# Attention of a hybrid decoder step: value products four units behind the scores, turns of `o` one round later, a negated maximum, q scaled in its copy

## The chip, the cores and the metric

The kernel runs on one core of a Trainium2 chip, as one program. The metric is the device time of one execution in microseconds. Three executions are given as their median. The chip has a matmul engine (TensorE, PE in the profile), a vector engine (VectorE, DVE), a scalar engine (ScalarE, ACT), a general one (GpSimd, POOL) and a queue engine (SyncE, SP) that issues most transfers. Each engine runs its own list of instructions in order; they wait for each other on semaphores.

## The reference

One inference step of a decoder with two layers, for a prompt of 1,024 tokens and 8 sample tokens. Layer A is an RWKV-7 mixing and an MLP; behind it shared keys and values are projected; layer B is a differential attention over them and an MLP. The part that matters here is the attention:

```python
def diff_combine(s, lam):
    p = jax.nn.softmax(s, axis=-1)
    return p[..., 0, :, :] - lam * p[..., 1, :, :]
# prompt: for each block i of 128 queries, 8 heads, two key maps of 64 each
s = jnp.einsum('bqhmd,bkhmd->bhmqk', qi, k).astype(jnp.float32) * ATTN_SCALE
s = jnp.where(k_pos[None, :] <= q_pos[:, None], s, NEG)
attn = diff_combine(s, lam).astype(v.dtype)
o = jnp.einsum('bhqk,bkhe->bqhe', attn, v)
# samples: one query each over 1,024 keys gathered by a page table, and the new key
on = of * lax.rsqrt(jnp.mean(jnp.square(of), -1, keepdims=True) + SUBLN_EPS) * g * (1.0 - lam_init)
```

`ATTN_SCALE` is 64 ** -0.5, that is 1/8, an exact power of two. All is float32.

## The kernel before, in words

The program is a row of phases with a barrier of all engines between them: start, projections, scan, sample scan, dense phase of layer 0 (which also projects k, v and q for the attention and writes them to a scratch in memory), attention, dense phase of layer 1. The change touches the dense phase in one place and `attention_phase`.

In the dense phase each projected tile of k, v or q (128 x 344) is copied out of PSUM by ACT at L1807 and sent to the scratch. There are 72 such copies, 24 of them of q.

In `attention_phase` the work of the prompt is cut into 64 units: unit u is head u // 8 and the query block `ORDER[u % 8]`, with `ORDER = (7, 0, 6, 1, 5, 2, 4, 3)`. A unit of block i has i + 1 key blocks of 128. So even units are long (8, 7, 6, 5 key blocks) and odd units short (1, 2, 3, 4), and each pair has nine. u % 8 is called r, the round within a head. Long and short units have PSUM and SBUF buffers of their own. All engines run the same loop over u, from 0 to `END` (74), and each does in round u what belongs to it:

- PE, round u: turn (transpose) the first four blocks of the combined attention of unit w = u - `LAG` (`turn4`, L2233), with `LAG = 3`; the scores of unit u (L2251) with the causal mask added by a matmul (L2255); the turn of the other blocks of w; the value products of w (`values`, L2265); and the extras of u.
- DVE, round u: the maximum of the scores of u (`maxima`, L2405) and, from it, the negated and scaled maximum `nb` (L2407); a page sum (L2424); `combine` of unit u - 1 (L2413, L2415, and the scalar_tensor_tensor L2419, which gives map 0 plus a ratio times map 1); in odd rounds a second page sum. At r = 5 the finished `o` of the head before is scaled (L2443).
- ACT, round u: copies of the turned blocks of w out of PSUM (`turned`, L2529), mixed with the two exponentials of unit u - 1 (`exps`, L2521, bias `nb`, scale 1/8, and the sum of the row); the copies of the extras; the copy of the value products of w into `o` (`take`, L2536) and its sum of squares (L2539). At r = 4 the square root for the head before (L2594), which needs a table load each way.
- POOL, round u: products of a page of sample keys with a query row (L2223), 64 pages in rounds 0 to 42, three in two rounds (one in an even round, two in an odd one). The first of a round waits until DVE has combined unit u - 2.
- SP: loads of key pages, of value pages, and of query rows (`q_row`, L2172), in order of rounds.

The extras (`extras`) are the remaining turns that go through the one turning bank of PSUM (`tb`): the rows of the next head's k and v at r = 2 to 5 ("rows"); the turns of the scaled `o` of the head before ("fin", two halves, L2233 on PE, L2550 on ACT), at r = 6 and 7 of the next head; the page scores (L2283) and what follows for the two halves of the samples, at u = 22 and 43 and some rounds behind; and the products with value pages (L2308, L2315) at eight values of u from 28 to 58. Each user of the bank waits until ACT has copied what the one before it put there; `nth` numbers them in the order of the loop.

```python
for u in range(END):
    w = u - LAG
    for i in range(2):
        for name in attn_rounds(w)[i:i + 1]:
            turned(name)
        if 1 <= u <= NU:
            exps(u - 1, (i,))
    for name in extras(u):
        extra(name)
    if 0 <= w < NU:
        take(w)
```

This is ACT's loop (L2579 to L2589).

## Time and profile before

| | |
|---|---|
| median of three runs | 3,694.8 us (3,684.2 to 3,699.2) |
| profiled execution | 3,698.0 us |
| its span | 3,696.2 us |
| PE busy | 3,319.3 us (90%) |
| DVE busy | 1,960.4 us (53%) |
| ACT busy | 1,443.6 us (39%) |
| POOL busy | 1,756.3 us (48%) |
| attention phase | from about 2,370 to 2,815 us of the span |

The profile is of one execution, taken by the hardware. Times in it count from the start of the span. "L2407" is line 2407 of the kernel. A busy share is a mean over phases with different limits, so each stage has to be read by itself. A row of waits says which engine and line stood idle and which instruction ended that, as far as semaphores tell it.

### The profile page before, as it was taken

How to read it: one execution, taken by the hardware profiler on the slowest of the kernel's cores; microseconds unless marked ns; L12 is line 12 of the kernel's file. 1: busy time of each engine (PE TensorE's matmuls, PEld its weight loads, DVE VectorE, ACT ScalarE, POOL GpSimd, SP SyncE). 2: the span in 40 equal slices, each digit the busy share in tenths (PEclk: the TensorE clock that was granted, in tenths of full speed). 3: DMA queues.
4: the chain of work that ended last, by engine and by line, in shares of the span. 5: the costliest groups of instructions: out<-in, count | busy, mean ns of one | idle time of the engine just before them, and what ended most of it. 6: DMA issues, size and time to landing. Idle time of an engine off the chain costs nothing. (4 is left out here: it accounts for less than half of the span.)

```text
span 3696.2 us, 78976 instructions
## 1 busy us (share of the span) xinstructions
PE 3319.3 (90%) x34073; PEld 3076.8 (83%) x34073; DVE 1960.4 (53%) x2233; ACT 1443.6 (39%) x2357; POOL 1756.3 (48%) x716
## 2 busy tenths in 40 slices
PE   7999879999985499999999999777886999999997
PEld 6889668888884499999999999654555999999997
DVE  6985264555532675673344342298744746742432
ACT  3433324433331234343333343355654443433332
POOL 3676410001000266666667666464402667666663
PEclk8999979999996699999999999888888999999998
DMA  8556533433432544545445566568755444444442
GB/s 289 173 168 181 171 109 114 133 129 112 133 96 61 183 136 132 143 139 153 140 140 155 156 199 188 179 225 272 276 180 161 132 137 143 137 144 140 138 146 84
DMA packets 784518, 575.27 MB, mean 156 GB/s; under 512 B 45306, under 2 KB 747666, under 8 KB 783916
## 3 DMA queue, kind: packets, MB, share of 16 engines
q1 hardware_dynamic: 728356, 506.07, 44.6%
q10 hardware_dynamic: 55816, 64.16, 5.3%
q8 instruction: 270, 4.42, 0.5%
q14 instruction: 76, 0.62, 0.1%
HBM read 499.86 MB, written 70.29 MB: 154 GB/s over the span
## 5 line engine op out<-in xcount | busy, mean ns | idle before, releaser
L1702 POOL TENSOR_TENSOR dense_w_lo<-w_raw,dense_w_hi 128x1024 fp32r<-128x1024 f32 x504 | 1290.8, 2566 | 985.4 <-ACT dense_w_hi L1785 985.2
L1754 PE MATMUL acc<-dense_x_hi,dense_w_hi 128*128 128x344 f32 x2496 | 792.7, 322 | 27.2 <-DVE dense_x_lo L1891 21.0
L1755 PE MATMUL acc<-dense_x_lo,dense_w_hi 128*128 128x344 f32 x2496 | 788.3, 320 | 0.0
L1785 ACT ACTIVATE dense_w_hi<-w_raw 128x1024 fp32r<-128x1024 f32 x504 | 530.6, 1056 | 510.6 <-PE acc L1759 443.8
L1754 PEld LDWEIGHTS acc<-dense_x_hi,dense_w_hi 128*128 128x128 f32 x2496 | 470.5, 188 | 33.5 <-DVE dense_x_lo L1891 16.6
L1754 PE MATMUL acc<-dense_hid_hi,dense_w_hi 128*128 128x344 f32 x1536 | 487.2, 322 | 0.0
L1755 PE MATMUL acc<-dense_hid_lo,dense_w_hi 128*128 128x344 f32 x1536 | 483.4, 319 | 0.0
L1755 PEld LDWEIGHTS acc<-dense_x_lo,dense_w_hi 128*128 128x128 f32 x2496 | 470.8, 189 | 0.6
L1759 PE MATMUL acc<-dense_x_hi,dense_w_lo 128*128 128x344 f32 x2496 | 447.2, 321 | 2.2 <-POOL dense_w_lo L1702 2.2
L1759 PEld LDWEIGHTS acc<-dense_x_hi,dense_w_lo 128*128 128x128 f32 x2496 | 407.2, 189 | 2.7 <-POOL dense_w_lo L1702 2.7
L797 POOL TENSOR_TENSOR x0T<-nT,levels 128x512 f32<-128x512 f32 x16 | 29.7, 1856 | 592.6 <-DVE bR L1296 592.6
L1907 DVE TENSOR_TENSOR dense_relu<-dense_relu 128x344 f32<-128x344 f32 x192 | 124.0, 646 | 338.7 <-ACT dense_relu L1801 338.7
L478 POOL TENSOR_TENSOR proj_w_lo<-proj_w_raw,proj_w_hi 128x1024 fp32r<-128x1024 f32 (+1 forms) x84 | 229.6, 2744 | 135.1 <-ACT proj_w_hi L598 82.2
L1754 PEld LDWEIGHTS acc<-dense_hid_hi,dense_w_hi 128*128 128x128 f32 x1536 | 288.5, 188 | 1.6
L1755 PEld LDWEIGHTS acc<-dense_hid_lo,dense_w_hi 128*128 128x128 f32 x1536 | 288.3, 188 | 1.6
L1759 PE MATMUL acc<-dense_hid_hi,dense_w_lo 128*128 128x344 f32 x1536 | 274.2, 321 | 0.0
L1801 ACT ACTIVATE dense_relu<-acc 128x344 f32<-128x344 f32 x192 | 88.0, 458 | 455.9 <-PE acc L1759 428.6
L1759 PEld LDWEIGHTS acc<-dense_hid_hi,dense_w_lo 128*128 128x128 f32 x1536 | 249.6, 188 | 0.0
L1926 DVE SCALAR_TENSOR_TENSOR z<-acc,mods,z 128x344 f32<-128x344 f32 (+1 forms) x144 | 81.0, 567 | 300.3 <-PE acc L1759 300.3
L506 PE MATMUL acc<-proj_x_hi,proj_w_hi 128*128 128x344 f32 (+2 forms) x672 | 214.3, 323 | 13.2 <-ACT proj_w_hi L598 8.8
L2223 POOL TENSOR_TENSOR att_k_prod<-att_k_page,att_q_row_all 128x1024 f32<-128x1024 f32 x64 | 150.1, 2359 | 154.8 <-DVE att_attn_short L2419 66.7
L507 PE MATMUL acc<-proj_x_lo,proj_w_hi 128*128 128x344 f32 (+2 forms) x672 | 213.6, 322 | 0.0
(406 smaller groups left out, 6097.1 us busy)
## 6 DMA issues: line engine op xcount, KB each, us to landing
w_raw<-in_ffn_w SPq DMA_DIRECT2D x384, 512.0 KB, 4.2
ada_quarter<-in_ada_w SPq DMA_DIRECT2D x40, 1024.0 KB, 10.9
proj_w_raw<-in_a_w_rkv SPq DMA_DIRECT2D x72, 512.0 KB, 4.1
att_k_page<-in_cache_k SPq DMA_DIRECT2D x64, 512.0 KB, 4.2
att_v_page<-in_cache_v SPq DMA_DIRECT2D x64, 512.0 KB, 6.0
scratch_mix<-proj_stage ACTq DMA_DIRECT2D x72, 344.0 KB, 3.1
scratch_mix<-dense_stage ACTq DMA_DIRECT2D x72, 172.0 KB, 2.1
w_raw<-in_a_w_o SPq DMA_DIRECT2D x24, 512.0 KB, 4.4
```

The costliest lines, as they stand in the source:

```text
L478: nc.gpsimd.tensor_tensor(wlo[:, s % NW, :, 0:w], raw[:, s % NRAW, :, 0:w], whi[:, s % NW, :, 0:w].bitcast(F32), ALU.subtract).then_inc(S( ...
L506: T_.matmul(out, whi[:, s % NW, k, 0:w], xh[x][:, k, :], start=k == 0, stop=False)
L507: T_.matmul(out, whi[:, s % NW, k, 0:w], xl[x][:, k, :], start=False, stop=False)
L1702: nc.gpsimd.tensor_tensor(wlo[:, i % NW], raw[:, i % NRAW], whi[:, i % NW].bitcast(F32), ALU.subtract).then_inc(S("lo"), 1)
L1754: T_.matmul(out, whi[:, s % NW, k, :], a, start=j.first and k == 0, stop=False)
L1755: T_.matmul(out, whi[:, s % NW, k, :], b, start=False, stop=False)
L1759: last = T_.matmul(out, wlo[:, s % NW, k, :], a, start=False, stop=j.last and k == KC - 1)
L1785: A(whi[:, i % NW], raw[:, i % NRAW], ACT.Copy).then_inc(S("hi"), 1)
L1801: A(t[:, n % 2, :], bank(jobs[s].acc), ACT.Relu).then_inc(S("taken"), 1)
L1907: V.tensor_tensor(tt, tt, tt, ALU.mult).then_inc(S("hid_sq"), 1)
L1926: V.scalar_tensor_tensor(zk, ps[:, 0:w], m.mod(gt, j.mo), zk, ALU.mult, ALU.add).then_inc(S("added"), 1)
L2223: nc.gpsimd.tensor_tensor(prod[:, j % NR, :], kp[:, j % NK, :], qb[:, b % 2, :], ALU.mult).then_inc(S("prod"), 1)
```

## The change

Four edits:

1. `LAG` goes from 3 to 4: turns and value products of a unit stand four rounds behind its scores.
2. The turns of the scaled `o` move from rounds 6 and 7 to round 7 and round 0 of the head after.
3. The maximum is written negated by the reduce itself, so the tensor_scalar that scaled and negated it, the buffer between them and its two factors go; the same for the samples' page scores.
4. q is multiplied by 1/8 when ACT copies it out of PSUM in the dense phase; the exponentials lose their scale.

```diff
--- before.py
+++ after.py
@@ -1804,7 +1804,7 @@
                     n = sum(1 for i in jobs[0:s] if i.kind in "kvq")
                     need(act, "mm", s + 1)
                     need(act, f"out{n % NOUT}", 16 * (n // NOUT))
-                    A(stage[:, n % NOUT, :], bank(j.acc), ACT.Copy).then_inc(S("taken"), 1)
+                    A(stage[:, n % NOUT, :], bank(j.acc), ACT.Copy, scale=ATTN_SCALE if j.kind == "q" else 1.0).then_inc(S("taken"), 1)
                     act.wait_ge(S("taken"), count[s])
                     nc.scalar.dma_start(m.scr[row[j.kind], j.mo, :, j.g * G:(j.g + 1) * G], stage[:, n % NOUT, :]
                                         ).then_inc(S(f"out{n % NOUT}"), 16)
@@ -2030,7 +2030,7 @@
         NK, NV, NR = 4, 12, 3
         GS, GR = NS // 2, NS // 2 * 16
         SM, VU = (22, 43), (28, 32, 36, 40, 49, 52, 55, 58)
-        END, LAG = NU + 10, 3
+        END, LAG = NU + 10, 4
         q, k, v = sb("q", [P, 2, SEQ]), sb("k", [P, 2, SEQ]), sb("v", [P, SEQ])
         krow, vrow = sb("k_rows", [P, KC, P]), sb("v_rows", [P, 2, KC, P])
         causal, mask, eyer = sb("causal", [P, P]), sb("causal_r", [P, P], F32R), sb("eye_r", [P, P], F32R)
@@ -2038,9 +2038,8 @@
         at = (sb("attn_long", [P, 2, SEQ]), sb("attn_short", [P, 2, SEQ // 2]))
         aT = (sb("attn_cols_long", [P, SEQ]), sb("attn_cols_short", [P, SEQ // 2]))
         o, osq, outT = sb("o", [P, 2, KC, P]), sb("o_sq", [P, P]), sb("out_cols", [P, SEQ])
-        mx, nb, l, rl, w1 = (sb(x, [P, 4, 2]) for x in ("max", "neg_max", "sums", "weights", "ratio"))
+        nb, l, rl, w1 = (sb(x, [P, 4, 2]) for x in ("neg_max", "sums", "weights", "ratio"))
         ss, rs, sums2 = sb("ss", [P, KC]), sb("rms", [P, KC]), sb("square_sums", [P, 2, KC])
-        factor = sb("score_factor", [P, 2])
         lq, eps, gcol = sb("lam_rows", [P, 2, P]), sb("eps", [P, 2]), sb("subln_g", [P, 2])
         ls, lam = sb("lam_sums", [P, 2]), sb("neg_lambda", [P, 1])
 
@@ -2108,8 +2107,10 @@
             out = []
             if 2 <= r <= 5 and h + 1 < NH:
                 out.append(("rows", h + 1, r - 2))
-            if r >= 6 and 1 <= h <= NH:
-                out.append(("fin", h - 1, r - 6))
+            if r == 7 and 1 <= h <= NH:
+                out.append(("fin", h - 1, 0))
+            if r == 0 and 2 <= h <= NH + 1:
+                out.append(("fin", h - 2, 1))
             g = group(u, 0)
             if g is not None:
                 out += [("page_sc", g, 0), ("page_sc", g, 1), ("page_new", g, 0)]
@@ -2367,9 +2368,6 @@
             V.tensor_copy(mask[:], causal[:]).then_inc(S("consts"), 1)
             V.tensor_copy(eyer[:], m.ident[:]).then_inc(S("consts"), 1)
             V.memset(eps[:, 0:1], SUBLN_EPS)
-            V.memset(factor[:, 0:1], -ATTN_SCALE).then_inc(S("factor"), 1)
-            V.memset(factor[:, 1:2], 1.0).then_inc(S("factor"), 1)
-            need(dve, "factor", 2)
             V.memset(eps[:, 1:2], P * SUBLN_EPS).then_inc(S("consts"), 1)
             V.memset(ones[:], 1.0)
             for i in range(4):
@@ -2402,9 +2400,7 @@
             def maxima(u):
                 c = u % 4
                 need(dve, "s_mm", u + 1)
-                V.tensor_reduce(mx[:, c, :], both_scores(u), AX.X, ALU.max).then_inc(S("max"), 1)
-                need(dve, "max", u + 1)
-                V.tensor_scalar(nb[:, c, :], mx[:, c, :], factor[:, 0:1], factor[:, 1:2], ALU.mult, ALU.mult).then_inc(S("nb"), 1)
+                V.tensor_reduce(nb[:, c, :], both_scores(u), AX.X, ALU.max, negate=True).then_inc(S("nb"), 1)
 
             def combine(u):
                 kd, c, n = kind(u), u % 4, blocks(u) * P
@@ -2445,9 +2441,7 @@
                 g = group(u, 1)
                 if g is not None:
                     need(dve, "t_in", nth["page_new", g, 0] + 1)
-                    V.tensor_reduce(pmx[0:GR, :], pr[0:GR, :], AX.X, ALU.max).then_inc(S("page_nb"), 1)
-                    need(dve, "page_nb", 2 * g + 1)
-                    V.tensor_scalar(pmx[0:GR, :], pmx[0:GR, :], -ATTN_SCALE, None, ALU.mult).then_inc(S("page_nb"), 1)
+                    V.tensor_reduce(pmx[0:GR, :], pr[0:GR, :], AX.X, ALU.max, negate=True).then_inc(S("page_nb"), 1)
                 g = group(u, 2)
                 if g is not None:
                     need(dve, "page_exp", g + 1)
@@ -2518,7 +2512,7 @@
                 need(act, "nb", u + 1)
                 need(act, "attn", u - 1)
                 for mp in maps:
-                    A(pm[kd][:, mp, 0:n], scores_of(u, mp), ACT.Exp, bias=nb[:, c, mp:mp + 1], scale=ATTN_SCALE,
+                    A(pm[kd][:, mp, 0:n], scores_of(u, mp), ACT.Exp, bias=nb[:, c, mp:mp + 1],
                       accum_out=l[:, c, mp:mp + 1]).then_inc(S("exp"), 1)
 
             def turned(name):
@@ -2594,8 +2588,8 @@
                     A(ss[:], sums2[:, (h - 1) % 2, :], ACT.Sqrt, bias=eps[:, 0:1], scale=1.0 / P).then_inc(S("rms"), 1)
                 g = group(u, 1)
                 if g is not None:
-                    need(act, "page_nb", 2 * g + 2)
-                    A(pr[0:GR, :], pr[0:GR, :], ACT.Exp, bias=pmx[0:GR, 0:1], scale=ATTN_SCALE, accum_out=pl[0:GR, 0:1]).then_inc(S("page_exp"), 1)
+                    need(act, "page_nb", g + 1)
+                    A(pr[0:GR, :], pr[0:GR, :], ACT.Exp, bias=pmx[0:GR, 0:1], accum_out=pl[0:GR, 0:1]).then_inc(S("page_exp"), 1)
             for name in ("k_out", "v_out", "mix_out"):
                 act.wait_ge(S(name), 16 * NH)
```

PE at the turn of `o` of head 1, rounds 22 and 23 (`att_attn_long` and `_short` are the combined attention of long and short units, `att_scores` the page scores, `att_o` the scaled `o`). Before:

```order
L2251 MATMUL acc<-att_k,att_q 128x512 x2
L2251 MATMUL acc<-att_k,att_q 128x128 x2
L2255 MATMUL acc<-att_causal_r,att_eye_r 128x128 x2
L2233 MATMUL aux<-ident,att_o 128x128 x4
L2265 MATMUL aux<-att_v_rows,att_attn_cols_short 128x128 x2
L2283 MATMUL aux<-ident,att_scores 64x128 x8
L2297 MATMUL aux<-att_ones,att_new_prod 64x1
L2233 MATMUL aux<-ident,att_attn_long 128x128 x4
L2251 MATMUL acc<-att_k,att_q 128x512 x2
L2255 MATMUL acc<-att_causal_r,att_eye_r 128x128 x2
```

After the change:

```order
L2252 MATMUL acc<-att_k,att_q 128x512 x2
L2252 MATMUL acc<-att_k,att_q 128x128 x2
L2256 MATMUL acc<-att_causal_r,att_eye_r 128x128 x2
L2234 MATMUL aux<-ident,att_attn_long 128x128 x3
L2266 MATMUL aux<-att_v_rows,att_attn_cols_long 128x128 x4
L2284 MATMUL aux<-ident,att_scores 64x128 x4
L2266 MATMUL aux<-att_v_rows,att_attn_cols_long 128x128 x3
L2284 MATMUL aux<-ident,att_scores 64x128 x4
L2298 MATMUL aux<-att_ones,att_new_prod 64x1
L2234 MATMUL aux<-ident,att_attn_short 128x128 x2
L2252 MATMUL acc<-att_k,att_q 128x512 x2
L2256 MATMUL acc<-att_causal_r,att_eye_r 128x128 x2
L2234 MATMUL aux<-ident,att_o 128x128 x4
```

The turn of `att_o` went from behind the scores of round 22 (512 and 128 columns) to behind those of round 23 (512 columns); the page scores now stand between the value products of a long unit, and the long scores of round 22 stand with long turns where they stood with short ones.

DVE in round 2 and the start of round 3. Before:

```order
L2405 TENSOR_REDUCE att_max<-acc 128x2
L2407 TENSOR_SCALAR att_neg_max<-att_max,att_score_factor 128x2
L2424 TENSOR_REDUCE att_scores<-att_k_prod 128x16
L2413 RECIPROCAL att_weights<-att_sums 128x2
L2415 TENSOR_SCALAR att_ratio<-att_weights,att_sums,att_neg_lambda 128x1
L2419 SCALAR_TENSOR_TENSOR att_attn_short<-att_probs_short,att_ratio 128x128
L2405 TENSOR_REDUCE att_max<-acc 128x2
L2407 TENSOR_SCALAR att_neg_max<-att_max,att_score_factor 128x2
```

After the change:

```order
L2403 TENSOR_REDUCE att_neg_max<-acc 128x2
L2420 TENSOR_REDUCE att_scores<-att_k_prod 128x16
L2409 RECIPROCAL att_weights<-att_sums 128x2
L2411 TENSOR_SCALAR att_ratio<-att_weights,att_sums,att_neg_lambda 128x1
L2415 SCALAR_TENSOR_TENSOR att_attn_short<-att_probs_short,att_ratio 128x128
L2403 TENSOR_REDUCE att_neg_max<-acc 128x2
L2420 TENSOR_REDUCE att_scores<-att_k_prod 128x16
```

The reduce writes `att_neg_max` itself, and one instruction of a unit is gone; the order of the others is the same.

ACT in rounds 11 and 12 (`att_k_rows` is the copy of an extra). Before:

```order
L2529 ACTIVATE att_attn_cols_long<-aux 128x512
L2521 ACTIVATE att_probs_long,att_sums<-acc,att_neg_max 128x896
L2529 ACTIVATE att_attn_cols_long<-aux 128x512
L2521 ACTIVATE att_probs_long,att_sums<-acc,att_neg_max 128x896
L2503 ACTIVATE att_k_rows<-aux 128x512
L2512 DMA out_k_prompt<-att_k_rows 128x8x128
L2536 ACTIVATE att_o<-aux,att_weights 128x128
L2539 ACTIVATE att_o_sq,att_square_sums<-att_o 128x128
L2529 ACTIVATE att_attn_cols_short<-aux 128x128
L2521 ACTIVATE att_probs_short,att_sums<-acc,att_neg_max 128x256 x2
```

After the change:

```order
L2523 ACTIVATE att_attn_cols_short<-aux 128x512
L2515 ACTIVATE att_probs_long,att_sums<-acc,att_neg_max 128x896 x2
L2497 ACTIVATE att_k_rows<-aux 128x512
L2506 DMA out_k_prompt<-att_k_rows 128x8x128
L2530 ACTIVATE att_o<-aux,att_weights 128x128
L2533 ACTIVATE att_o_sq,att_square_sums<-att_o 128x128
L2523 ACTIVATE att_attn_cols_long<-aux 128x512
L2515 ACTIVATE att_probs_short,att_sums<-acc,att_neg_max 128x256
L2523 ACTIVATE att_attn_cols_long<-aux 128x512
L2515 ACTIVATE att_probs_short,att_sums<-acc,att_neg_max 128x256
```

Before, the copies of long turned blocks stood between long exponentials and the short copy before short ones; now the short copy stands before the long exponentials, and the long copies between short ones.

## Rows read from the trace of the kernel before

**Rows 1.** Busy time by stretch: busy us and instructions of each engine, PE clock, DMA.

```profile
2390.00:2430.00 40.00, 30.94 (x164) 21.80 (x164) 39.20 (x48) 21.22 (x61) 25.96 (x12) 0.79 0.65 220
2430.00:2480.00 50.00, 36.88 (x197) 25.79 (x197) 47.09 (x58) 30.91 (x81) 28.04 (x12) 0.83 0.65 219
2730.00:2780.00 50.00, 44.45 (x295) 30.00 (x296) 23.97 (x42) 29.20 (x81) 0.00 (x0) 0.90 0.51 161
```

**Rows 2.** Groups and waits of the attention phase: busy, mean ns; waited us, times, longest us.

```profile
L2407 DVE TENSOR_SCALAR att_neg_max<-att_max,att_score_factor 128x2 f32<-128x2 f32 x64 | 43.2, 674 | 2.3
...
DVE att_max L2405 <- PE acc L2255: 18.8, 9, 6.1
...
PE aux L2233 <- DVE att_o L2443: 14.1, 3, 7.9
...
DVE att_max L2405 <- PE acc L2255: 54.0, 15, 7.7
...
PE aux L2233 <- ACT att_attn_cols_long L2529: 8.0, 5, 3.4
...
PE aux L2233 <- DVE att_o L2443: 1.0, 1, 1.0
```

**Rows 3.** Timeline, units 11 to 13: start, us, engine, line, out<-in [idle before <-releaser].

```profile
2449.19 1.21 DVE L2424 TENSOR_REDUCE att_scores<-att_k_prod 128x16 f32<-128x1024 f32 x1
...
2450.32 1.74 DVE L2405 TENSOR_REDUCE att_max<-acc 128x2 f32<-128x1536 f32 x1
...
2452.10 0.29 DVE L2407 TENSOR_SCALAR att_neg_max<-att_max,att_score_factor 128x2 f32<-128x2 f32 x1
2452.30 1.21 DVE L2424 TENSOR_REDUCE att_scores<-att_k_prod 128x16 f32<-128x1024 f32 x1
...
2454.58 4.66 POOL L2223 TENSOR_TENSOR att_k_prod<-att_k_page,att_q_row_all 128x1024 f32<-128x1024 f32 x2 [2.79 <-DVE att_attn_short L2419]
...
2455.31 1.64 DVE L2407 TENSOR_SCALAR att_neg_max<-att_max,att_score_factor 128x2 f32<-128x2 f32 x1
...
2456.96 1.22 DVE L2424 TENSOR_REDUCE att_scores<-att_k_prod 128x16 f32<-128x1024 f32 x1
...
2458.60 1.46 DVE L2419 SCALAR_TENSOR_TENSOR att_attn_long<-att_probs_long,att_ratio 128x768 f32<-128x768 f32 x1
```

**Rows 4.** Timeline, units 22 and 23.

```profile
2513.70 1.12 PE L2233 MATMUL aux<-ident,att_o 128*128 128x128 f32 x4 [7.85 <-DVE att_o L2443]
...
2517.70 4.64 POOL L2223 TENSOR_TENSOR att_k_prod<-att_k_page,att_q_row_all 128x1024 f32<-128x1024 f32 x2 [5.13 <-DVE att_attn_short L2419]
...
2523.67 1.23 DVE L2405 TENSOR_REDUCE att_max<-acc 128x2 f32<-128x1024 f32 x1 [6.14 <-PE acc L2255]
...
2526.76 0.88 DVE L2419 SCALAR_TENSOR_TENSOR att_attn_long<-att_probs_long,att_ratio 128x640 f32<-128x640 f32 x1
```

**Rows 5.** Timeline, units 27, 28 and 30.

```profile
2552.39 1.65 DVE L2407 TENSOR_SCALAR att_neg_max<-att_max,att_score_factor 128x2 f32<-128x2 f32 x1
...
2554.08 0.47 ACT L2521 ACTIVATE att_probs_short<-acc,att_neg_max 128x256 f32<-128x256 f32 x1 [2.10 <-DVE att_neg_max L2407]
...
2555.64 1.92 PE L2308 MATMUL aux<-att_v_page,att_page_attn 128*32 128x512 f32 x16 [2.14 <-ACT att_v_rows L2508]
...
2574.72 1.49 DVE L2405 TENSOR_REDUCE att_max<-acc 128x2 f32<-128x1280 f32 x1 [2.33 <-PE acc L2255]
```

**Rows 6.** Query rows: issue on SP's queue, and POOL's products behind them.

```profile
2500.81 0.43 SPq L2172 DMA_DIRECT2D att_q_row_all<-scratch_sample_y  x1
...
2507.89 4.67 POOL L2223 TENSOR_TENSOR att_k_prod<-att_k_page,att_q_row_all 128x1024 f32<-128x1024 f32 x2 [2.52 <-issue]
...
2589.43 2.36 POOL L2223 TENSOR_TENSOR att_k_prod<-att_k_page,att_q_row_all 128x1024 f32<-128x1024 f32 x1 [5.90 <-DMA att_q_row_all<-scratch_sample_y]
```

**Rows 7.** Timeline, unit 42.

```profile
2654.84 2.02 DVE L2405 TENSOR_REDUCE att_max<-acc 128x2 f32<-128x1792 f32 x1 [2.08 <-PE acc L2255]
```

**Rows 8.** The copies of k, v and q out of PSUM, by tile.

```profile
L1807 ACT ACTIVATE dense_stage<-acc x72: 435/457/459, 2086.6 to 2356.1; 128x344 f32<-128x344 f32 x72
```

## The prediction

> **What bounds the kernel now.** I read the instruction times around the changed lines first. All of the change but one scale factor lies in the attention phase, from about 2,370 to 2,815 us of the span. Then the busy time by stretch [rows 1]: from 2,390 to 2,480 us DVE is busy 86.3 of 90 us, while PE has 67.8. From 2,730 to 2,780 us it is the other way round: PE 44.5 of 50, DVE 24.0. So there are two regimes. Units 1 to 42, while the sample group's pages are multiplied on POOL and summed on DVE, are limited by DVE; units 43 to 63 by PE together with ACT, which empties PE's one turning bank.
>
> The waits [rows 2] say where each regime leaks. With pages, DVE waits 18.8 us for scores, and PE waits 14.1 us for the scaled `o` (three times, 7.9 us at the longest). Without pages DVE waits 54.0 us for scores, but PE waits only 8.0 us for the turned long columns on ACT and 1.0 us for `o`: DVE's wait there is spare time.
>
> The timeline of units 11 to 13 [rows 3] shows what ends DVE's idle time inside its own instructions. The tensor_scalar on L2407 has 2 elements a partition. In unit 12 it takes 0.29 us. In unit 13 it takes 1.64 us, from 2,455.31 to 2,456.95, and POOL's product, begun at 2,454.58, lasts half of 4.66 us, to 2,456.91. The combine of unit 12 (L2419, 768 elements) starts at 2,458.60 and ends at 2,460.06, after POOL's second product (2,459.24). So a DVE operation of this kind does not run beside a product; it ends after it. And the page sum (L2424) at 2,456.96 reads that very product.
>
> **The change, part by part.** The profiled execution took 3,698.0 us, its span 3,696.2; the sum is made against 3,698.0, 3.2 above the median of 3,694.8.
>
> *The negated maximum* removes 64 instructions of L2407, 43.2 us of busy time, 674 ns each [rows 2]. The upper bound is all of that, if DVE were the limit everywhere and nothing took its place. The lower is zero. What stays depends on the unit. In an even unit (long scores) the product was finished before, so the page sum moves up. It starts 1.98 us after a 1.74 us reduce at 2,450.32 [rows 3]; after an instruction that it need not wait for, a reduce starts 0.08 us before the other's end (1.13 us behind one of 1.21, at 2,449.19). Without L2407 that is 1.66, a gain of 0.3 us. In an odd unit DVE waits for the same product with or without the tensor_scalar, and its next combine waits for POOL's second one: no gain on DVE. There `nb` comes 1.4 to 2 us earlier, which only ACT sees. There are 21 even units with pages. In five of them (10, 16, 20, 32, 36) the gain is taken back by the query row that POOL needs for the next sample: it is issued only after the last product but one. Issued at 2,500.81 it is followed by POOL's product at 2,507.89, 7.1 us later, and at 2,589.43 POOL had waited 5.9 us on it [rows 6]. That leaves 16 x 0.3 = **4.8 us**. In the last 21 units DVE has 54 us spare [rows 2]: 0.
>
> The Trainium skill (SBUF — State Buffer, two separate sides) says that DVE and GpSimd hold their common pair of ports under a lock for a whole instruction and the loser "fully blocks". By that rule the trace agrees (1.64 us instead of 0.29). Its plain reading would let the blocking vanish with the blocked instruction; that is rival E.
>
> *The later turns of `o`*. In unit 22 PE waits until 2,513.70 with the first half, then still has values, page scores and a turn to do, and the scores of unit 23 reach DVE at 2,523.67, after 6.14 us of idle time [rows 4]. After the change the first turn stands behind the scores of unit 23, and those can be done before 2,517.5. POOL's two products (from 2,517.70, 4.64 us) still end at 2,522.34, and the combine, which took until 2,527.64, then ends 0.9 us behind them, at 2,523.3: **4.3 us**. Unit 15 had the same wait with 1.9 us, but there POOL's products and the next query row end at the same time as before: 0.2. In the last 21 units the wait was 1.0 us [rows 2]: **1.0**.
>
> *One more unit between scores and values*. (a) The turn no longer waits for the combine; in the DVE regime that only moves PE's idle time. (b) Pairing: before, ACT had long turns and long exponentials in the same round, now long turns meet short exponentials, and PE gets long scores with long turns. Work is the same, so I take a third of the 8.0 us that PE waited for the long columns in the last 21 units [rows 2]: **2.7 us**. Ends: -3 (if PE's light rounds now wait for ACT instead) and 8. (c) The end of the phase has one unit more to drain, about 2 us of PE work, and the scores of unit 63 stand as much earlier: 0.
>
> *Both together, at page products of PE*. In unit 27 `nb` ends at 2,554.04 behind POOL; ACT waits 2.10 us for it, PE 2.14 us for ACT, and the chain of page values behind it runs into DVE at unit 30, which waits 2.33 us [rows 5]. With `nb` 1.6 us earlier that is **1.6 us**. Units 39, 41 and 42 wait 0.7, 1.3 and 2.1 us for scores (the last in [rows 7]); half of that, **2.1**. Unit 37 gains 0.7, as POOL's query row is late there.
>
> *q scaled in ACT's copy* (24 of the 72 of L1807, 457 ns each [rows 8]): the same instruction with another constant, so 0; each waits for PE anyway. Two memsets and a wait at the start go: POOL's first row is what is waited for: 0.
>
> Sum: 4.8 + 4.3 + 0.2 + 1.0 + 2.7 + 1.6 + 2.1 + 0.7 = 17.4 us, 3,698.0 to 3,680.6; against the median, **3,677.4 us**, 0.5% faster.
>
> **The rivals.**
> *A, handed back.* The gains before unit 32 end in waits for query rows and pages, and PE's light rounds wait for ACT as long as before. For it: the 5.9 us on a query row [rows 6], which no part of the change issues earlier. Against it: unit 23 has no such wait behind it. It leaves unit 23 and part of the even units, 4.3 + 2.7 = 7 us: 3,688.
> *B, PE gets faster too.* The granted clock was 0.79 to 0.83 with pages and 0.90 without [rows 1], of levels at 1.2 and 2.4 GHz, and PE had stood idle for up to 7.9 us before the slow pieces. If PE idles less and 0.90 becomes 0.97 in the 135 us after unit 43, of which PE is busy nine tenths, that is 0.07 x 120 = 8 us; with all 8.0 instead of 2.7 us of waits, 5 more: 31 us in all, 3,664. The Trainium skill (TensorE: Matmul & The Clock Gate, Part 1) ties the half clock to an idle PE; the low figure beside the 7.9 us wait fits that. Against it: the page values make PE wait for ACT in any order.
> *C, slower.* PE has its long scores, turns and values now in the same round. In units 43 to 63 the odd unit's scores come some 1.5 us later (four turns, up to eight value matmuls), while ACT's long exponentials, which follow them, hold the turning bank's next copy. If neither is made up in the even round, 10 pairs x 1.5 = 15 us are lost; where pages meet them too, only the 4.8 us of the even units stay: 10 us slower, 3,705. It decides once DVE, with 54 us spare in 135, uses that up; that speaks against it.
> *E, the blocking goes.* The 43.2 us hold 64 x 0.29 = 18.6 us of work and 24.7 us of waiting for POOL. If DVE could use the odd units' share, the time would be 3,677 - 25 = 3,653. Against it: the page sum of 2,456.96 needs the product that ended at 2,456.91 [rows 3].
> *D, it does nothing*, because every removed wait had another behind it: 3,695.
>
> **How the numbers follow.** Forecast 0.47, A 0.22, B 0.15, C 0.07, D 0.06, E 0.03. A measurement of this kernel tells about 0.5%, 18.5 us, from no change. The forecast lies just inside it: with its bounds (12 to 24 us) it is over in 0.20 of its 0.47, and B and E are over, so faster 0.38. C gives slower 0.05, the rest is 0.57. The range goes from B to between D and A: **3,663 to 3,692**.
>
> **What would show it.** Right: L2407's group gone and DVE busy some 40 us less; in units 22 and 23 no wait of PE for `o` over 1 us and unit 23's reduce within 5 us of unit 22's combine; in odd units with pages the page sum still begins as POOL's product ends, in even ones 0.3 us sooner after the reduce; query rows still waited for. Wrong: a time under 3,664 with the page units shorter by far more than 13 us, which means the blocking did go; or new waits of DVE for odd scores after unit 43.

## The result, and the profile after

The changed kernel took **3,705.5 us** (median of 15 runs, 3,690.7 to 3,711.7), the kernel before, measured beside it, 3,690.8 (15 runs, 3,680.5 to 3,699.2): ratio 1.0027, 95% interval 1.0014 to 1.0039, so 5 to 14 us slower, a small difference but clear of the interval. The forecast was 3,677.4, and the time lies outside its range. The profiled execution took 3,707.4 us with a span of 3,705.6.

The length of the attention phase says more than the whole time. I count it from unit 0's maximum to the next phase's first operation on POOL, and cut it at the maxima of units 22, 43 and 63. First the kernel before, in this cut (columns: stretch, its length, busy us and instructions of PE, PE's weight load, DVE, ACT, POOL, then PE's granted clock as a share of 2.4 GHz (0.50 is the half clock), DMA share, GB/s):

```profile
2374.60:2513.60 139.00, 98.26 (x521) 67.40 (x518) 121.62 (x146) 77.51 (x201) 79.46 (x34) 0.81 0.73 243
2513.60:2659.00 145.40, 119.82 (x727) 78.01 (x727) 118.84 (x149) 83.22 (x219) 70.69 (x30) 0.86 0.84 305
2659.00:2792.30 133.30, 109.72 (x683) 72.58 (x683) 63.23 (x117) 83.29 (x213) 0.00 (x0) 0.88 0.41 133
2792.30:2816.60 24.30, 9.94 (x63) 8.16 (x61) 6.42 (x13) 11.99 (x31) 0.00 (x0) 0.78 0.14 45
```

The changed kernel, same view and cut:

```profile
2382.60:2517.50 134.90, 92.59 (x518) 64.39 (x516) 100.13 (x124) 76.20 (x198) 80.11 (x34) 0.81 0.77 251
2517.50:2660.90 143.40, 117.17 (x709) 78.92 (x708) 102.12 (x126) 81.39 (x216) 71.42 (x30) 0.83 0.86 311
2660.90:2798.20 137.30, 112.10 (x695) 74.90 (x694) 57.89 (x96) 82.64 (x214) 0.00 (x0) 0.86 0.38 127
2798.20:2827.40 29.20, 12.45 (x74) 10.16 (x72) 6.12 (x12) 15.25 (x37) 0.00 (x0) 0.76 0.12 38
```

442.0 us became 444.8. The first two stretches won 4.1 and 2.0 us, the third lost 4.0, the drain (what is left to do behind unit 63's maximum) lost 4.9. L2407 is gone, as forecast (page: DVE 1,960.4 us busy before, 1,905.2 after, 55 less where some 40 were expected). Behind unit 22 this helped little or not at all, and PE's clock fell there: 0.86 and 0.88 became 0.83 and 0.86.

Attention began 8.0 us later, at 2,382.6, though nothing ahead of it is changed but a factor in the copies of q. From 1,320 us of the first trace to the last of these copies the distance of the two traces stays 8.3 us, so the copies themselves are no slower with the factor.

The local steps of the forecast are there. DVE's waits for scores in the stretch with pages (up to unit 43's maximum) and in the one without, against [rows 2]:

```profile
DVE att_neg_max L2403 <- PE acc L2256: 27.0, 11, 4.6
...
DVE att_neg_max L2403 <- PE acc L2256: 60.6, 19, 7.4
```

No wait of PE for `o` is left in either stretch (14.1 us in three [rows 2]), but DVE waits for scores 27.0 us instead of 18.8 with pages, and 60.6 us in 19 waits instead of 54.0 in 15 without: the new waits after unit 43 that the prediction named as a sign of being wrong. Units 22 and 23, against [rows 4]:

```profile
2517.49 1.48 DVE L2403 TENSOR_REDUCE att_neg_max<-acc 128x2 f32<-128x1280 f32 x1
...
2521.30 4.67 POOL L2224 TENSOR_TENSOR att_k_prod<-att_k_page,att_q_row_all 128x1024 f32<-128x1024 f32 x2 [4.81 <-DVE att_attn_short L2415]
...
2521.78 0.62 PE L2234 MATMUL aux<-ident,att_o 128*128 128x128 f32 x4
...
2521.98 1.23 DVE L2403 TENSOR_REDUCE att_neg_max<-acc 128x2 f32<-128x1024 f32 x1 [0.85 <-PE acc L2256]
...
2525.32 1.33 DVE L2415 SCALAR_TENSOR_TENSOR att_attn_long<-att_probs_long,att_ratio 128x640 f32<-128x640 f32 x1
```

The 6.14 us wait is 0.85 us, and the turn of `o` comes at the full clock (0.62 us, before 1.12). In unit 12 the page sum starts 1.66 us after the reduce (1.98 before), just as forecast. In odd units POOL's product ends the page sum's wait, where L2407 used to sit, as forecast from [rows 3] (unit 13):

```profile
2459.79 4.66 POOL L2224 TENSOR_TENSOR att_k_prod<-att_k_page,att_q_row_all 128x1024 f32<-128x1024 f32 x2 [2.47 <-DVE att_attn_short L2415]
2462.17 1.22 DVE L2420 TENSOR_REDUCE att_scores<-att_k_prod 128x16 f32<-128x1024 f32 x1 [1.68 <-POOL att_k_prod L2224]
```

### The profile page after: what moved, and what is told of

Same layout as the page of the kernel before. It is cut to its first block and busy times, and to the rows that moved or that the text cites. A ratio compares the mean times of both kernels' runs of the same rounds, so it can differ in the third digit from the quotient of the medians.

```text
span 3705.6 us, 78908 instructions
## 1 busy us (share of the span) xinstructions
PE 3323.2 (90%) x34073; PEld 3083.7 (83%) x34073; DVE 1905.2 (51%) x2165; ACT 1443.0 (39%) x2357; POOL 1758.4 (47%) x716
## 5 line engine op out<-in xcount | busy, mean ns | idle before, releaser
L478 POOL TENSOR_TENSOR proj_w_lo<-proj_w_raw,proj_w_hi 128x1024 fp32r<-128x1024 f32 (+1 forms) x84 | 228.8, 2735 | 139.8 <-ACT proj_w_hi L598 85.4
```

What stands on the lines that cost most here:

```text
L478: nc.gpsimd.tensor_tensor(wlo[:, s % NW, :, 0:w], raw[:, s % NRAW, :, 0:w], whi[:, s % NW, :, 0:w].bitcast(F32), ALU.subtract).then_inc(S( ...
```

## The experiments

Twelve edited kernels, and a second profile of the kernel before, of the changed one and of the changed one with three units. "Before" in the ratios was run beside each. "Half clock", in us, is worked out from the granted clock in stretches of 2 us: two times (1 - clock) times the length, summed; where the stretches begin shifts it by up to 2 us. "PE busy" and "half clock" are those of units 22 to 63.

| kernel | ratio to before (95%) | attention | units 0-22 | 22-43 | 43-63 | drain | PE busy 22-63 | half clock 22-63 |
|---|---|---|---|---|---|---|---|---|
| before | 1 | 442.0 | 139.0 | 145.4 | 133.3 | 24.3 | 229.5 | 72.5 |
| before, again | | 442.6 | 139.8 | 146.2 | 131.1 | 25.5 | 228.8 | 69.9 |
| changed | 1.0027 (1.0014-1.0039) | 444.8 | 134.9 | 143.4 | 137.3 | 29.2 | 229.3 | 85.4 |
| changed, again | | 445.4 | 135.5 | 143.4 | 137.3 | 29.2 | 229.2 | 85.4 |
| negated maximum alone | 0.998 (0.997-0.9991) | 428.2 | 136.0 | 139.5 | 127.2 | 25.5 | 223.4 | 55.8 |
| turns of o alone | 0.9967 (0.9949-0.9984) | 427.3 | 137.9 | 138.0 | 126.0 | 25.4 | 218.3 | 58.1 |
| four units alone | 1.002 (1.0011-1.003) | 451.1 | 138.3 | 145.0 | 137.3 | 30.5 | 231.0 | 87.2 |
| changed, three units | 0.9961 (0.9947-0.9974) | 422.7 | 137.3 | 133.6 | 127.3 | 24.5 | 216.7 | 52.7 |
| changed, three units, again | | 419.5 | 135.5 | 132.7 | 126.1 | 25.2 | 214.5 | 51.3 |
| changed, five units | 0.9985 (0.997-0.9999) | 433.6 | 134.4 | 133.0 | 132.0 | 34.2 | 218.7 | 54.6 |

Two theories to begin with: 1, the fourth unit costs; 2, the phases ahead of attention were made longer.

**The parts apart.** `lag3_in_after`:

```diff
-        END, LAG = NU + 10, 4
+        END, LAG = NU + 10, 3
```

> The changed kernel with three units between scores and values again; the negated maximum, the scaled q and the later turns of o stay. Theory 1 (the fourth unit costs: units 37 to 63 lost 7 us against before, and the drain behind the last combine lasts 12.2 instead of 7.2 us): the attention phase becomes 10 to 14 us shorter than in the changed kernel, the drain is 7.2 us again, and the time is 5 to 12 us below the kernel before, ratio 0.997 to 0.999. Theory 2 (the loss lies in the 8 us by which the phases ahead of attention were longer, through the scaled copy of q or through where the instructions lie): these stay, and the time is that of the changed kernel less the 5 us of the drain, ratio 1.001 to 1.002.

Measured: 14 us faster than before, more than theory 1 wanted; attention 22 us shorter than changed (expected 10 to 14). Only the drain missed theory 1: by its count, from the last combine to the reciprocal, 8.4 us instead of 7.2. `lag4_alone` is the opposite edit (3 to 4) in the kernel before:

> The kernel before with four units between scores and values, nothing else. Theory 1: 8 to 14 us slower than before (drain 5, the last 27 units 7, nothing won with pages), ratio 1.002 to 1.004; unit 63's scores and all of units 43 to 63 come late by some 0.3 us a unit. Theory 2: only the drain's 5 us, and the phases ahead of attention as in the kernel before: ratio 1.0013.

7.4 us slower, and 8.8 us more attention (451.1 against 442.3, the mean of the two profiles before), 5.6 of them in the drain: about what theory 1 expected. `fin_alone` takes only the hunk of `extras` into the kernel before:

> The kernel before with only the two turns of o one round later. Both theories: unit 23's scores are no longer waited for 6 us, which was worth 5.6 us in the changed kernel; 3 to 6 us faster than before, ratio 0.9985 to 0.999. If the query rows hand it back, 0 to 2 us.

It won 12 us by the ratio and 15 in attention: twice the upper end of what was expected, and more than twice the forecast's 5.5 us. `max_alone` is the changed kernel with LAG 3 and the old hunk of `extras`:

> The kernel before with only the maximum written negated and q scaled in its copy. Theory 1: 3 to 6 us faster than before, all of it by unit 42, nothing after; phases ahead of attention unchanged within a few us of scatter. Theory 2: if the scaled copy of q (or the code's place) makes the phases ahead of attention longer, they are 5 to 8 us longer than in the kernel before, and the time is 2 to 4 us slower.

7 us faster, attention 14 us shorter. So two of the three parts are good. The third loses more than both win, but only beside them: changed with three units against changed is 22 to 26 us of attention, where the same edit in the kernel before cost 8.8. What the fourth unit mostly does is to take back what the other two won. About half of their excess over the forecast stands in units 43 to 63, for which the forecast had 0 and 1.0 us: 127 and 126 us instead of 131 and 133.

**Scatter.** Both kernels, unedited, once more:

> The kernel before, profiled once more, to see how far two executions of one program lie apart stage by stage. If the phases ahead of attention scatter by themselves, they differ by up to 10 us from the first profile (2,376.9 us), and the 8 us by which the changed kernel came to attention later are scatter. In the attention phase (439.7 us in the first) theory 1 wants 430 to 442 us.

> The changed kernel, profiled once more. Theory 1: the attention phase (443.3 us in the first profile) is again over 440 us, and TensorE's time at half clock in units 43 to 63 again near 38 us (it was 17 to 24 us in the three kernels that keep three units and carry one or both of the other parts).

Attention repeats to 0.7 us in both, that of the kernel with three units to 3.2 (its second profile, below). The phases ahead of it do not: attention began at 2,374.6 and 2,384.7 us in one kernel, 2,382.6 and 2,377.1 in the other. The 8 us are no more than this scatter. Over all profiles attention begins at 2,378.3 us in the mean of the four without the scaled q and at 2,377.7 in that of the thirteen with it; theory 2 falls. (The two expectations count attention from later operations, 2.3 and 1.5 us behind unit 0's maximum; by this count it took about 440 and 444 us, inside theory 1's bands.) In the changed kernel units 43 to 63 have 37.6 us at half clock both times, as expected.

**Parity or distance.** The busy time of PE differs by 13 us between three and four units, for the same instructions. With three units, long turns meet short scores; with four, long scores; with five, short ones again. `lag5`, with row buffers of the sums and weights for eight units:

```diff
-        END, LAG = NU + 10, 4
+        END, LAG = NU + 10, 5
-        nb, l, rl, w1 = (sb(x, [P, 4, 2]) for x in ("neg_max", "sums", "weights", "ratio"))
+        nb, l, rl, w1 = (sb(x, [P, 8, 2]) for x in ("neg_max", "sums", "weights", "ratio"))
...
-                need(dve, "take", u - 3)
+                need(dve, "take", u - 7)
```

> The changed kernel with five units between scores and values (row buffers of the sums for eight units). Turned values of a long unit then stand beside the scores of a short one again, as with three. Theory P (what costs is that long turns, long scores and long values share a round, parity): units 43 to 63 take 126 to 130 us as with three units, TensorE is at half clock 17 to 26 us of it, the drain becomes 17 us; time 5 to 12 us below the changed kernel. Theory Q (more distance itself costs, whatever the parity): 137 us or more, drain 17 us, time 5 to 15 us above the changed kernel.

Units 22 to 43 took 133.0 us as with three, so distance itself costs nothing there. Units 43 to 63 took 132.0, between the theories, with 31 us at half clock instead of 17 to 26. The drain grew by five more: 24.9, 29.2, 34.2 us with three, four, five units. In all, five units won back 11.5 us of the 24 of attention. `lag5` also has deeper row buffers, but these were not what cost: in the changed kernel DVE's waits in units 22 to 63 end with scores, exponentials, products of POOL and once, after 0.2 us, its own ratio, never with a value product, its copy or a turn.

**Page steps.** Where the page steps stand, four units put the extra steps of the page group beside a short unit. One round later they meet a long one again:

```diff
-        SM, VU = (22, 43), (28, 32, 36, 40, 49, 52, 55, 58)
+        SM, VU = (23, 44), (29, 33, 37, 41, 50, 53, 56, 59)
```

> The changed kernel (four units) with the steps of the sample group's page values and of its page scores one round later each (table of rounds 23, 44 and 29, 33, 37, 41, 50, 53, 56, 59), so that they meet a unit of the same kind between turns as they did with three. Length of attention is counted here from unit 0's maximum to the next phase's first operation on POOL: 442.0 and 442.6 us before, 444.8 and 445.5 changed, 422.7 with three units. Theory P (with four, page steps meet the light round of a short unit; PE waits 2 to 4.5 us there and its clock stays at half through the long round that follows): units 22 to 63 take 262 to 270 us instead of 280.7, half clock 55 to 65 instead of 85 us, the drain stays at 29; attention 427 to 434 us. Theory Q (four units cost by the long turns and long scores in one round, wherever the page steps stand): 278 us or more, attention 442 to 448.

> As above, but only the page values' rounds are later by one. Theory P: units 28 to 42 and 49 to 60 gain (together 5 to 12 us against the changed kernel), the loss at units 45 to 47 behind the page scores' exponential (8 us against three units) stays. Theory Q: nothing over 3 us.

> The reverse: three units, and the page steps one round later. Theory P: the page steps now meet short units there, and attention is 6 to 15 us longer than 422.7 us (with three units and the old rounds), with more than 65 us of half clock in units 22 to 63. Theory Q: within 4 us of 422.7.

| kernel | ratio (95%) | attention | 0-22 | 22-43 | 43-63 | drain | PE busy 22-63 | half clock |
|---|---|---|---|---|---|---|---|---|
| pages later | 0.9996 (0.9982-1.0011) | 438.6 | 135.5 | 142.3 | 133.3 | 27.5 | 217.7 | 57.8 |
| values later (one run) | | 438.8 | 136.1 | 139.6 | 134.0 | 29.2 | 220.4 | 66.6 |
| three units, pages later (one run) | | 431.1 | 135.5 | 142.3 | 128.3 | 25.0 | 222.8 | 71.4 |
| four, then three units | 0.9998 (0.9981-1.0015) | 437.4 | 135.3 | 142.7 | 135.1 | 24.3 | 227.5 | 77.3 |

The direction is theory P's both times: 6 us better with four units, 8 to 12 worse with three. The size is theory P's with three units only; with four, attention stays above its 427 to 434 us. In pages_later PE's half clock came down as expected and its busy time with it, but its idle time rose from 51.4 to 57.9 us. Moving the page values alone won as much (438.8 us; 5.3 us in units 28 to 42, 0.5 in 49 to 60). So where the steps stand is a quarter to a half of the loss, not the whole. `lag4_then_3` returns to three units once the pages are done (of its diff only the table of units is shown):

```diff
+        def units_of(u):
+            return [u - 4] if u < 43 else [39, 40] if u == 43 else [u - 3]
```

> The changed kernel with four units up to round 42, two units' values in round 43, and three from there. Theory P: units 22 to 43 stay at 143 us, units 43 to 63 fall from 137 to 127 to 131 us, the drain from 29.2 to 24.5; attention 430 to 434 us, 12 to 15 us below the changed kernel. If the loss after unit 43 came from what the page part left behind, units 43 to 63 stay at 135 us or more and only the drain's 5 us come back.

The drain's 5 us came back, but units 43 to 63 took 135.1 us: as it was put, theory P missed, and the other reading, something left behind by the page part, is not refuted. A reading made afterwards speaks against it. Round 43 does two units, and unit 44 is 4.1 us later than in the changed kernel; from there to unit 63 this kernel lost 2.4 us against the first profile with three units, the changed kernel 8.9. No run separates the two.

**Waits or clock.** Where does PE's busy time go? This is PE in the changed kernel, units 29 and 30:

```profile
2569.24 3.57 PE L2316 MATMUL aux<-att_fold,att_page_o 128*128 128x1 f32 x16 [2.73 <-ACT att_v_rows L2502]
...
2573.17 1.09 PE L2234 MATMUL aux<-ident,att_attn_long 128*128 128x128 f32 x4 [0.36 <-ACT att_res L2565]
...
2574.19 2.51 PE L2252 MATMUL acc<-att_k,att_q 64*128 64x512 f32 x8
```

PE waits 2.73 us behind a short unit's two value matmuls, and then everything up to the long scores runs at 1.2 GHz: 16 one-column matmuls 3.57 us, four turns 1.09, the long scores 2.51. The single wait does not decide it. With three units the waits just ahead of the same column matmuls are 0.86 and 1.34 us in both profiles, and the matmuls took 3.41 us in one and 2.17 in the other; the two units took 16.7 and 14.8 us, a large part of what these two profiles differ by. In the changed kernel PE waits like this ahead of the columns in units 29 and 37 (2.73 and 2.07 us) and once later, in unit 53; in units 24 and 45 it waits 4.5 and 3.9 us. `filled` puts matmuls whose result nobody reads into units 24 and 45, in a free part of the value bank:

```diff
+                if group(u, 2) is not None:
+                    need(pe, "take", w)
+                    for i in range(5):
+                        T_.matmul(ob[:, P:4 * P], m.ident[:], k[:, (u // KC) % 2, 0:3 * P], start=True, stop=True)
```

> The changed kernel with five matmuls of 384 columns (about 3.2 us at the full clock, results unused) on TensorE in units 24 and 45, where it waits 3.9 us for ACT's exponential of the page scores. Theory C (the fall of the clock behind the wait costs): in unit 45 to 47, which were at 0.60 and 0.71, the clock stays above 0.9, and units 45 to 48 become 3 to 5 us shorter; time 3 to 8 us below the changed kernel. Theory W (the wait costs and the clock does not matter): those units are as long or 0 to 3 us longer, the time not shorter.

`filled_more` adds four of them before the page columns where r = 5:

```diff
+                    if name[0] == "page_cols" and u % KC == 5:
+                        for i in range(4):
+                            T_.matmul(ob[:, P:4 * P], m.ident[:], k[:, (u // KC) % 2, 0:3 * P], start=True, stop=True)
```

> As the kernel filled, and four more unused matmuls of 384 columns ahead of the page columns in units 29, 37 and 53, where TensorE with four units waits 2.7, 2.1 and 2.7 us for ACT's copy of v's rows. Theory C (waits cost through the clock behind them): the two stretches at half clock behind units 29 and 37, 10 and 13 us long, shrink by more than half, units 29 to 45 become 3 to 6 us shorter than in filled, TensorE's busy time for the program's own work falls with them; attention 435 to 439 us. Theory W (only the waits count): units 29 to 45 as in filled (142.8 us for units 22 to 43) or longer by up to 1.5 us.

> The changed kernel with three units and with the five unused matmuls in units 24 and 45, where TensorE still waits 3.7 and 3.4 us. Theory C: half clock in units 22 to 63 falls from 52.7 to 35 to 45 us and attention from 422.7 to 417 to 421 us, ratio to before 0.994 to 0.996. Theory W: 422 to 425 us.

> The changed kernel with three units, profiled once more: attention within 1 us of 422.7 us if the phase repeats as the other two kernels' did (442.0 and 442.6; 444.8 and 445.5), and units 22 to 63 with 50 to 56 us of half clock.

| kernel | ratio (95%) | attention | 0-22 | 22-43 | 43-63 | drain | PE busy 22-63 | half clock |
|---|---|---|---|---|---|---|---|---|
| filled | 0.9989 (0.9972-1.0006) | 441.8 | 134.9 | 142.9 | 136.5 | 27.5 | 230.7 | 71.6 |
| filled more | 0.9978 (0.996-0.9997) | 432.5 | 135.7 | 136.0 | 133.3 | 27.5 | 226.7 | 40.9 |
| three units, filled | 0.9959 (0.9943-0.9975) | 421.0 | 135.6 | 133.2 | 127.8 | 24.4 | 219.9 | 42.3 |

The same three steps in filled_more:

```profile
2554.12 2.75 PE L2368 MATMUL aux<-att_k,ident 128*128 128x384 f32 x8
...
2557.02 1.95 PE L2316 MATMUL aux<-att_fold,att_page_o 128*128 128x1 f32 x16
...
2559.32 0.63 PE L2234 MATMUL aux<-ident,att_attn_long 128*128 128x128 f32 x4 [0.36 <-ACT att_res L2572]
2559.88 1.35 PE L2252 MATMUL acc<-att_k,att_q 64*128 64x512 f32 x8
```

Units 29 and 30 as a whole, in filled and in filled_more (one row each):

```profile
2561.90:2578.20 16.30, 12.34 (x64) 9.62 (x65) 10.70 (x14) 9.08 (x25) 3.28 (x2) 0.69 0.95 334
```

```profile
2552.50:2565.20 12.70, 11.26 (x71) 8.14 (x72) 10.60 (x13) 9.09 (x25) 3.30 (x2) 1.00 0.91 314
```

More work, and 3.6 us sooner. Units 45 and 46, in the changed kernel and in filled:

```profile
2674.70:2693.00 18.30, 12.83 (x56) 8.79 (x57) 7.30 (x14) 12.34 (x31) 0.00 (x0) 0.65 0.11 30
```

```profile
2671.60:2685.90 14.30, 11.42 (x67) 7.38 (x66) 7.09 (x14) 11.82 (x30) 0.00 (x0) 1.00 0.14 38
```

4.0 us shorter, at the full clock (units 45 to 47 together 18.5 us instead of 22.9, as theory C expected). In unit 24 the filling brought next to nothing. The clock rose from 0.57 to 0.96 there, but what PE won ended in a wait of 2.13 us for DVE's weighted page scores, and in unit 25 the clock was 0.50 both times. Units 22 to 43 had 10 us less half clock and took 0.5 us less, so half clock is not lost time everywhere. And filled as a whole gained only 3 us of attention: units 53 to 60 gave back 5.4 us, since another wait of 2.7 us, in unit 53, now brought the clock down for longer (units 53 and 54 at 0.60 instead of 0.78). With that wait and those of units 29 and 37 filled too, the gain stays. Attention falls from 444.8 to 432.5 us, and of the 226.7 us that PE is busy in units 22 to 63 16.3 are the unused matmuls (6.9 us in units 24 and 45, 9.4 ahead of the page columns), so the program's own work took 210 us instead of 229. In the timed runs it is 0.2% faster than before where the changed kernel is 0.3% slower. Theory C is shown for the waits that were filled: more work on PE, and less time. It does not explain the whole loss: with 40.9 us at half clock, fewer than with three units, filled_more still needs 11.4 us more attention than they do (2.6 in the drain, 9.4 in units 22 to 63). With three units there is little left to fill: 421.0 us is inside theory C's band, but between 422.7 and 419.5 us of the unfilled kernel (expected to repeat within 1 us), and says nothing. Its ratio is that of the plain version: **the changed kernel with three units, at 0.9961, beats both kernels**, and needs no filling.

## Why the prediction was wrong

**The step that failed is "One more unit between scores and values", (b) and (c).** It gave a gain of 2.7 us for the pairing (ends -3 and 8) and 0 for the drain; together they cost 24 us. Against the mean of the two profiles with three units (421.1 us), the changed kernel's 445.1 is 24.0 longer:

- units 22 to 43: 10.2 us, units 43 to 63: 10.6 us. PE's busy time rose from 215.6 to 229.3 us for the same instructions, 13.7 us, its idle time by 7.1.
- the drain: 4.3 us. There is no POOL, no page and no score left to overlap: in every round PE turns, ACT copies, PE multiplies, ACT copies. The last combine and the reciprocal of the last head's root in the changed kernel:

```profile
2804.75 0.75 DVE L2415 SCALAR_TENSOR_TENSOR att_attn_short<-att_probs_short,att_ratio 128x512 f32<-128x512 f32 x1
...
2816.99 0.20 DVE L2437 RECIPROCAL att_rms<-att_ss 128x8 f32<-128x8 f32 x1 [10.45 <-ACT att_ss L2588]
```

and with three units:

```profile
2768.72 0.75 DVE L2415 SCALAR_TENSOR_TENSOR att_attn_short<-att_probs_short,att_ratio 128x512 f32<-128x512 f32 x1
...
2777.11 0.20 DVE L2437 RECIPROCAL att_rms<-att_ss 128x8 f32<-128x8 f32 x1 [6.60 <-ACT att_ss L2588]
```

12.2 against 8.4 us. "The scores of unit 63 stand as much earlier" was the wrong half of (c): its maximum came 415.6 us after unit 0's, with three units 398.2 and 394.3. And the other half was too small: 4.3 us, not about 2.
- units 0 to 22: 1.2 us won.

I took a third of 8.0 us of waits, as if the work were only shared out anew. PE's waits in units 43 to 63 with three units and with four (us, times, longest):

```profile
PE aux L2234 <- ACT att_attn_cols_long L2523: 7.8, 6, 3.4
```

```profile
PE aux L2234 <- ACT att_attn_cols_short L2523: 4.9, 2, 3.9
...
PE acc L2252 <- ACT att_probs_long L2515: 3.0, 2, 2.2
PE aux L2316 <- ACT att_v_rows L2502: 2.7, 1, 2.7
```

PE's idle time in this stretch is no shorter, 25.2 us instead of 21.1 and 19.7, and its waits stand elsewhere, in rounds that are light for PE, right ahead of a long unit's turns, scores and values in one.

Without this step the forecast's terms add up to 14.7 us, and the changed kernel with three units was 14 us faster. That is partly luck: by the timed runs the two parts alone won 7 and 12 us, and the terms for units 43 to 63 were far too small.

**Negated maximum, 4.8 us, with 1.6 + 2.1 + 0.7 where both parts meet.** Right in mechanism before unit 43: with that part alone, the even units 8, 10, 12, 18 and 20 each gain 0.3 us. Alone it won 14.1 us of attention (442.3, the mean of two, to 428.2), 9.7 of them before unit 43, beside 9.2 for the four terms. "In the last 21 units 0" was wrong: 5.0 us, where DVE has time to spare but the clock was 0.93 instead of 0.88 to 0.90.

**Later turns of o, 4.3 + 0.2 + 1.0.** In unit 23 it won 6.2 us and gave 1.6 back by unit 24, so 4.6: right. Unit 15's 2.0 us were down to 0.4 by unit 17, about as forecast. The 1.0 in the last units was 6.2 us, again with a higher clock (0.91). The two parts are not additive (14.1 and 15.0 us alone, 21.2 together), and neither are their gains of half clock (15 and 13 us alone, 19 together, from 71).

**q scaled in the copy, 0.** Right for the copies, whose distance in the two traces did not change.

**The rivals.** C gave 3,705 a chance of 0.07, and that is the time, in part by luck: C expected 15 us lost after unit 43 and 5 won, and in the traces units 43 to 63 lost 5, the drain, which C did not count, 4.3, and the rest of attention won 6.6. Its mechanism is half there: long scores, turns and values of PE in the same round, new waits of DVE for scores. But against three units they cost as much before unit 43 as after, and two thirds of that loss (13.7 of 20.8 us) stands in PE's busy time at the lower clock, which C did not have. B had the right lever (clock x busy time) and the wrong sign for this change; with three units it happened in part (0.91 after unit 43, where B had 0.97). The Trainium skill (TensorE: Matmul & The Clock Gate, Part 1) ties half clock to an idle PE; the trace agrees on the direction, but here waits of 2.1 and 2.7 us, in rounds with little else on PE, went ahead of half clock. With three units waits of 0.86 and 1.34 us did, too, in one of two profiles. (Behind the 7.9 us wait of the kernel before, from 2,513.7 to 2,516.0, the clock was 0.50; the 0.79 to 0.83 that the prediction puts beside it are of stretches ahead of that wait.) A, D and E are out by the time; E's blocking time turned into explicit waits for POOL (1.68 us in unit 13).

**What stays open.** The traces give the changed kernel 2.8 us more attention than before, the timed runs 5 to 14 us more in all. With the two good parts alone and with both, too, the timed runs gain some 3 to 7 us less than attention does, and no run says where. The phases ahead of attention scatter by 25 us over the profiles (attention begins between 2,364.9 and 2,390.2), which hides a shift of a few us. What makes up the rest of the fourth unit's cost, beyond the drain, the rounds of the page steps and the filled waits, is not separated. Nor is it shown why pages_later has 6.5 us more idle time on PE.

## What to carry to other kernels

Cost a new order of the work also by how evenly it loads TensorE: for each of its waits, ask what it runs before and after, because the same matmuls cost nearly twice as much behind a thin round. A pipeline one stage deeper pays its drain at the end of the phase: 4.3 to 5.6 us here, where it bought 1.2 us in units 0 to 22. And when a change has three parts, time them apart: here two good ones were hidden by the third.

## What was not expected of the hardware

- Unused work made the kernel faster: 22 matmuls that nobody reads, 16 us of PE time, shortened attention by 12.3 us (filled_more).
- Sixteen one-column matmuls took 1.95 us at the full clock and 3.57 at the half; the scores of unit 30 (64x512, x8) 1.35 and 2.51.
- Attention, with all its waits and DMAs, repeats to 0.7 us in the kernel before and in the changed one, its time at half clock included (85.4 us both times in the changed one), while the phases ahead of it differ by 10 us between two executions of the kernel before. With three units it repeats only to 3.2 us: the same matmuls behind the same waits were granted the half clock in one profile and a higher one in the other.
